# Weight sums of the gate/up turns made by GpSimd additions in place of DVE additions

## The chip, the cores and the metric

The kernel runs on one core of a Trainium2 chip. The metric is the device time of one execution in microseconds (us). TensorE (PE in the profile) multiplies, ScalarE (ACT) and VectorE (DVE) prepare operands, GpSimd (POOL) starts some transfers and does small work, SyncE (SP) starts the loads of the weights.

## The reference, cut to what matters

The model has two layers over 256 tokens of width 2048: a pooling mixer and a SwiGLU FFN, then attention and a SwiGLU FFN. All is float32. The change touches only the two large products of each FFN, gate and up, each 2048 by 5632:

```python
def swiglu(x, wg, wu, wd):
    return (jax.nn.silu(x @ wg) * (x @ wu)) @ wd
...
h = h + swiglu(rmsnorm(h, ffn_norm[layer]), w_gate[layer], w_up[layer], w_down[layer])
```

## The kernel before, in words

**Products in three passes.** Each float32 weight tile is split: ACT rounds it into `w_hi` (L771), DVE subtracts that from the tile and writes the rest into `w_lo` (L1238), and PE makes hi by hi, lo by hi and hi by lo, one matmul of 512 columns each. The tile of one such step is 128 x 1024 and is called a unit. `w_hi` and `w_lo` are rings of `RING` = 4 units: ACT may round unit n when PE has finished unit n - 4 (`unit_used`), DVE follows ACT (`hi_ready`), PE follows DVE (`unit_ready`).

**Turns.** Columns of gate and up are worked off in 11 blocks of 512. Nine of them in each layer (18 in all) are "sum turns". For two sets s = 0 and 1 of the inner dimension a turn uses a seven-product scheme of the Strassen kind: some products take sums of weight halves instead of the halves themselves. A turn has 22 units in the fixed order below, counted from 0. A unit named `gate` or `up` is plain and costs PE 12 matmuls, every other unit costs 6: 180 matmuls in a turn.

```python
SUM_ORDER = [("B11", 0), ("B11", 1), ("B21", 0), ("gate", 4), ("B21", 1), ("gate", 5), ("B22", 1), ("T1", 1),
             ("B22", 0), ("T1", 0), ("gate", 6), ("gate", 7), ("T3", 0), ("T2", 1), ("T4", 0), ("T2", 0), ("T4", 1),
             ("up", 5), ("T3", 1), ("up", 4), ("up", 6), ("up", 7)]
T_SUMS = [("T2", 1), ("T2", 0), ("T4", 0), ("T4", 1)]
```

**The four sums of a set.** The first, T1, and the third, T3, are made by transfers that accumulate, which GpSimd starts (L2084 and L2087). The second is T2 = T1 + B22 and is written over T1; the fourth is T4 = B21 + T2 and is written over B21. Both are DVE additions of 128 x 1024 elements, from `raw` into `raw` (`weight_sum`, L1223 for T2 and L1227 for T4). DVE's own program places them: T2 of set 1 after unit 7, T2 of set 0 after unit 10, T4 of set 0 after unit 11, T4 of set 1 after unit 14. ACT waits on the semaphore `t_sum` before it rounds units 13 (T2, 1), 14 (T4, 0), 15 (T2, 0) and 16 (T4, 1).

**The other work of DVE in a turn.** It transposes the block before (`quad_turn`), combines PSUM banks (L1261 to L1297), and makes the low part of the activations (`act_lo`). GpSimd has no work in a turn but the four starts of transfers. SP's loads wait on `unit_ready` of the last unit that reads a slot of `raw`.

Of the kernel before, what the change touches and what calls it, by code (L numbers as in the profile page):

```python
# [28 lines left out]
ALU = mybir.AluOpType  # L29
# [45 lines left out]
SUM_TURNS = NFB - 2  # L75
# [146 lines left out]
AT = {u: n for n, u in enumerate(SUM_ORDER)}  # L222
# [20 lines left out]
def turn_half(form, n):  # L243

    if form in ("gate", "up"):
        return SLOT[form, n // 2], UNITS_D[n][2]
    slot = (SLOT_U if form in ("T3", "B22") else SLOT_G)[n]
    return slot, 2 * C if form in ("B21", "T4", "B22") else 0
# [33 lines left out]
def trunk(nc, x, pool_w, pool_rows, pool_scale, w_kv, w_q, w_o, w_gate, w_up, w_down, final_norm,  # L282
# [12 lines left out]
    with ExitStack() as ctx:  # L295
# [99 lines left out]
        def sem(name):  # L395
            return ctx.enter_context(nc.semaphore(name))
# [3 lines left out]
        unit_ready = sem("unit_ready")  # L400
# [11 lines left out]
        t_sum = sem("t_sum")  # L412
        t1_in = [sem(f"t1_in{n}") for n in range(SUM_SETS)]
# [65 lines left out]
        def sum_units(l, j):  # L479
            return (LAP_GU[l] + 2).units(SUM_UNITS * (j - 1))  # L480
# [6 lines left out]
        def steps_of(j, n):  # L487
            return 1 if j < SUM_TURNS or n + 1 < SUM_UNITS else 1 + SUM_STEPS - SUM_UNITS * SUM_TURNS
# [3 lines left out]
        def sum_done(l, j, unit):  # L492
            return len(T_SUMS) * (SUM_TURNS * l + j - 1) + T_SUMS.index(unit) + 1
# [519 lines left out]
        def _(ve):  # L1013
# [103 lines left out]
            def up_out(l, j):  # L1117
                job = JOB_GU[l] + 2 * j + 1
                pair = (JOB_GU[l] + 1) % 2
                ve.wait_ge(unit_used, turn_lap(l, j).units(2 * UD))  # L1120
                ve.wait_ge(job_out, job)
                for t in range(T):
                    last = nc.vector.scalar_tensor_tensor(out=act[:, t, :], in0=acc[:, 2 * pair + t, :],
                                                          scalar=r[:, t:t + 1], in1=act[:, t, :],
                                                          op0=ALU.mult, op1=ALU.mult)
                last.then_inc(job_out, 1)
# [87 lines left out]
            def weight_half(unit):  # L1214
                slot, off = turn_half(*unit)
                return raw[:, slot, off:off + 2 * C]

            def weight_sum(l, j, form, s):

                c = SUM_TURNS * l + j - 1  # L1220
                if form == "T2":
                    ve.wait_ge(t1_in[s], 16 * (c + 1))
                    nc.vector.tensor_tensor(weight_half(("T2", s)), weight_half(("T1", s)), weight_half(("B22", s)),  # L1223
                                            ALU.add).then_inc(t_sum, 1)
                else:
                    ve.wait_ge(t_sum, sum_done(l, j, ("T2", s)))
                    nc.vector.tensor_tensor(weight_half(("T4", s)), weight_half(("B21", s)), weight_half(("T2", s)),  # L1227
                                            ALU.add).then_inc(t_sum, 1)

            def sum_turn(l, j):  # L1230

                before = sum_units(l, j)
                c = SUM_TURNS * l + j - 1
                gate = JOB_GU[l] % 2
                for n, unit in enumerate(SUM_ORDER):
                    ve.wait_ge(hi_ready, before + n + 1)
                    w = (before + n) % RING
                    nc.vector.tensor_tensor(w_lo[:, w, :], weight_half(unit), w_hi[:, w, :].bitcast(F32),  # L1238
                                            ALU.subtract).then_inc(unit_ready, steps_of(j, n))
                    if n == 2 and j > 1:  # L1240
                        common_up(l, j - 1)
                    if n == 3:
                        if j > 1:
                            common_out(l, j - 1)
                        else:
                            up_out(l, j - 1)
                        quad_turn(l, j - 1, 0)
                    if n == 5:
                        quad_turn(l, j - 1, 1)
                    if n == 7:  # L1250
                        weight_sum(l, j, "T2", 1)
                    if n == 10:
                        weight_sum(l, j, "T2", 0)
                    if n == 11:
                        weight_sum(l, j, "T4", 0)
                    if n == 14:
                        weight_sum(l, j, "T4", 1)
                    if n == 15:
                        ve.wait_ge(unit_used, before + AT["gate", 7] + 1)
                        ve.wait_ge(p1_copied, c + 1)  # L1260
                        nc.vector.tensor_tensor(act[:, 0, :], pair_bank(gate, 0), common[:, 0, :],  # L1261
                                                ALU.add).then_inc(common_step, 1)
                    if n == 17:
                        ve.wait_ge(unit_used, before + AT["T2", 0] + 1)
                        ve.wait_ge(common_step, 4 * c + 1)
                        nc.vector.tensor_tensor(common[:, 0, :], acc[:, P6, :], common[:, 0, :],
                                                ALU.add).then_inc(common_step, 1)
                    if n == 19:
                        act_lo(l, j - 1)
                    if n == 20:  # L1270
                        ve.wait_ge(unit_used, before + AT["T3", 1] + 1)
                        ve.wait_ge(common_step, 4 * c + 2)
                        nc.vector.tensor_tensor(common[:, 1, :], acc[:, P7, :], common[:, 0, :],
                                                ALU.add).then_inc(common_step, 1)
                    if n == 21:
                        ve.wait_ge(unit_used, before + AT["T4", 1] + 1)
                        ve.wait_ge(common_step, 4 * c + 3)
                        nc.vector.tensor_tensor(act[:, 1, :], pair_bank(gate, 1), common[:, 1, :],
                                                ALU.add).then_inc(gate_sum, 1)
                        ve.wait_ge(gate_sum, c + 1)  # L1280
                        nc.vector.tensor_tensor(common[:, :, :], acc[:, P5:P5 + 1, :].to_broadcast([P, T, C]),
                                                common[:, :, :], ALU.subtract).then_inc(sums_free, 1)

            def common_up(l, j):

                ve.wait_ge(unit_used, sum_units(l, j + 1))
                ve.wait_ge(sums_free, (SUM_TURNS + 1) * l + j + 1)
                up = (JOB_GU[l] + 1) % 2
                nc.vector.tensor_tensor(common[:, :, :], acc[:, 2 * up:2 * up + 2, :], common[:, :, :],
                                        ALU.add).then_inc(common_step, 1)  # L1290

            def common_out(l, j):

                ve.wait_ge(common_step, 4 * (SUM_TURNS * l + j))
                ve.wait_ge(job_out, JOB_GU[l] + 2 * j + 1)
                for t in range(T):
                    last = nc.vector.scalar_tensor_tensor(out=act[:, t, :], in0=common[:, t, :],  # L1297
                                                          scalar=r[:, t:t + 1], in1=act[:, t, :],
                                                          op0=ALU.mult, op1=ALU.mult)
                last.then_inc(job_out, 1)  # L1300
# [163 lines left out]
            for j in range(1, NFB - 1):  # L1464
                sum_turn(0, j)
# [580 lines left out]
        def _(gp):  # L2046
# [26 lines left out]
            def turn_sums(l):  # L2073

                def half(form, s):
                    slot, off = turn_half(form, s)
                    return raw[:, slot, off:off + 2 * C]

                for j in range(1, NFB - 1):
                    before, c = sum_units(l, j), SUM_TURNS * l + j - 1  # L2080
                    for s in (1, 0):
                        gp.wait_ge(unit_ready, before + AT["B11", s] + 1)
                        gp.wait_ge(raw_in[SLOT_U[s]], 16 * sum_loads(l, j, "up", s))
                        gp.dma_start(half("T1", s), half("T3", s), accum_op=ALU.add).then_inc(t1_in[s], 16)  # L2084
                    for s in (0, 1):
                        gp.wait_ge(t1_in[s], 16 * (c + 1))
                        gp.dma_start(half("T3", s), half("B22", s), accum_op=ALU.add).then_inc(t3_in[s], 16)  # L2087

            def rotate(z, heads, n):

# [79 lines left out]
```

## Time and profile before

| what | value |
| --- | --- |
| median of 3 runs | 1667.57 us (1667.55 to 1669.52) |
| the profiled execution, its own time | 1667.48 us |
| its span, first to last instruction | 1665.7 us |
| TensorE busy in the span | 1650.5 us |
| DVE busy | 1414.6 us |
| ACT busy | 1115.3 us |
| GpSimd busy | 96.4 us |
| mean granted TensorE clock | 0.998 |

The 1.8 us between span and time lie around the program. The profiled execution stands 0.09 us under the median. Busy time counts overlapping instructions of an engine once. A timeline row that ends in "x2" is two instructions of one line merged; its duration is the time that the two together cover. Where an engine was idle before a row, the bracket says how long and what ended it.

### The profile page before, as it was taken

To read this page: it belongs to the slowest core of one execution; us is meant where nothing else is said; L and a number is where in the kernel's file an instruction comes from. 1 tells how busy PE (TensorE), PEld (TensorE's weight loads), DVE (VectorE), ACT (ScalarE), POOL (GpSimd) and SP (SyncE) were. 2 spreads that over 40 slices of the span, in tenths; PEclk is the share of its full clock that TensorE was granted. 3 is DMA by queue.
4 is the path that set the end of the run, shared out by engine and by line. 5 is a ranking of instruction groups with operands and counts; after the bars stand their busy time and mean duration, and the time that the engine had idled before them with its cause. 6 is when DMAs were issued, how large, how long until landed. Compare 5 with 4: busy or idle time off the path is not lost.

```text
span 1665.7 us, 19672 instructions
## 1 busy us (share of the span) xinstructions
PE 1650.5 (99%) x7492; PEld 1358.3 (82%) x7492; DVE 1414.6 (85%) x1582; ACT 1115.3 (67%) x1575; POOL 96.4 (6%) x126
## 2 busy tenths in 40 slices
PE   9999999999999999999999999999999999999998
PEld 8878888888888888888777887888888888888887
DVE  7879999999968988867676867999999996889887
ACT  6667777777766555546665565777777776655554
POOL 1100000000000000002011000000000000000000
PEclk9999999999999999999999999999999999999999
DMA  8568888888865565655434556888888887557564
GB/s 294 187 190 258 269 261 261 259 261 260 237 232 172 184 228 190 213 201 179 150 127 152 177 186 193 252 252 253 254 257 259 262 259 249 160 195 236 168 212 167
DMA packets 173590, 364.73 MB, mean 219 GB/s; under 512 B 6708, under 2 KB 6836, under 8 KB 173368
## 3 DMA queue, kind: packets, MB, share of 16 engines
q1 hardware_dynamic: 162832, 324.67, 57.1%
q0 software_dynamic: 10368, 37.75, 12.0%
q8 instruction: 59, 0.97, 0.2%
q10 hardware_dynamic: 296, 1.06, 0.2%
q14 instruction: 35, 0.29, 0.1%
HBM read 323.61 MB, written 2.10 MB: 196 GB/s over the span
## 4 chain that ended last, share of the span: by engine, by line
PE 94%; DMA 2%; DVE 2%; ACT 1%; issue 0%; SPq 0%; ACTq 0%
PE acc L1779 8%; PE acc L1781 8%; PE acc L1780 8%; PE acc L1656 7%; PE acc L1658 7%; PE acc L1657 7%; PE acc L1877 7%; PE acc L1878 7%; PE acc L1879 7%; PE acc L1794 6%; PE acc L1792 6%; PE acc L1793 6%; PE acc L1863 2%; PE acc L1864 2%; PE acc L1862 2%; DMA raw<-w_gate_in 1%
## 5 line engine op out<-in xcount | busy, mean ns | idle before, releaser
L1238 DVE TENSOR_TENSOR w_lo<-raw,w_hi 128x1024 fp32r<-128x1024 f32 x396 | 472.1, 1216 | 41.0 <-ACT w_hi L771 37.1
L771 ACT ACTIVATE w_hi<-raw 128x1024 fp32r<-128x1024 f32 x396 | 412.6, 1058 | 116.4 <-PE acc L1781 59.6
L826 ACT ACTIVATE w_hi<-raw 128x1024 fp32r<-128x1024 f32 x215 | 227.5, 1061 | 190.7 <-PE acc L1879 124.1
L1416 DVE TENSOR_TENSOR w_lo<-raw,w_hi 128x1024 fp32r<-128x1024 f32 x215 | 260.5, 1221 | 60.0 <-ACT w_hi L826 54.8
L1779 PE MATMUL acc<-w_hi,xT_hi 128*128 128x512 f32 x576 | 225.0, 391 | 3.9 <-DVE w_lo L1238 3.9
L1780 PE MATMUL acc<-w_lo,xT_hi 128*128 128x512 f32 x576 | 224.8, 390 | 0.0
L1781 PE MATMUL acc<-w_hi,xT_lo 128*128 128x512 f32 x576 | 224.6, 390 | 0.0
L1877 PE MATMUL acc<-w_hi,hT_hi 128*128 128x512 f32 x488 | 190.1, 390 | 0.3 <-DVE w_lo L1416 0.3
L1879 PE MATMUL acc<-w_hi,hT_lo 128*128 128x512 f32 x488 | 189.8, 389 | 0.0
L1878 PE MATMUL acc<-w_lo,hT_hi 128*128 128x512 f32 x488 | 189.8, 389 | 0.0
L1019 DVE TENSOR_TENSOR w_lo<-raw,w_hi 128x1024 fp32r<-128x1024 f32 x104 | 127.4, 1232 | 66.3 <-ACT w_hi L626 66.1
L1656 PE MATMUL acc<-w_hi,xT_hi 128*128 128x512 f32 x416 | 164.2, 395 | 0.0
L1658 PE MATMUL acc<-w_hi,xT_lo 128*128 128x512 f32 x416 | 162.1, 390 | 0.0
L1657 PE MATMUL acc<-w_lo,xT_hi 128*128 128x512 f32 x416 | 161.9, 389 | 0.0
L626 ACT ACTIVATE w_hi<-raw 128x1024 fp32r<-128x1024 f32 x104 | 108.9, 1062 | 73.2 <-PE acc L1658 56.1
L668 ACT ACTIVATE hT_f<-quad 32x256 f32<-32x256 f32 x320 | 132.8, 415 | 16.0 <-DVE quad L1180 11.2
L1779 PEld LDWEIGHTS acc<-w_hi,xT_hi 128*128 128x128 f32 x576 | 108.5, 188 | 27.4 <-DVE w_lo L1238 4.9
L1780 PEld LDWEIGHTS acc<-w_lo,xT_hi 128*128 128x128 f32 x576 | 108.5, 188 | 22.6
L1781 PEld LDWEIGHTS acc<-w_hi,xT_lo 128*128 128x128 f32 x576 | 108.6, 188 | 22.6
L1792 PE MATMUL acc<-w_hi,s_hi 128*128 128x512 f32 x288 | 112.0, 389 | 0.0
L1793 PE MATMUL acc<-w_lo,s_hi 128*128 128x512 f32 x288 | 112.0, 389 | 0.0
L1794 PE MATMUL acc<-w_hi,s_lo 128*128 128x512 f32 x288 | 112.0, 389 | 0.0
(202 smaller groups left out, 2751.7 us busy)
## 6 DMA issues: line engine op xcount, KB each, us to landing
raw<-w_gate_in SPq DMA_DIRECT2D x88, 1024.0 KB, 7.4
raw<-w_up_in SPq DMA_DIRECT2D x88, 1024.0 KB, 5.3
raw<-w_down_in SPq DMA_DIRECT2D x88, 1024.0 KB, 5.1
raw<-raw POOLq DMA_DIRECT2D x72, 512.0 KB, 5.2
raw<-w_q_in SPq DMA_DIRECT2D x16, 1024.0 KB, 5.1
raw<-w_o_in SPq DMA_DIRECT2D x16, 1024.0 KB, 5.0
raw<-w_kv_in SPq DMA_DIRECT2D x4, 1024.0 KB, 5.3
raw<-pool_w_in SPq DMA_DIRECT2D x3, 1024.0 KB, 13.9
```

Source lines behind the costliest of these rows:

```text
L771: nc.scalar.activation(w_hi[:, (before + n) % RING, :], raw[:, slot, off:off + 2 * C], ACT.Copy).then_inc(hi_ready, steps_of(j, n))
L1238: nc.vector.tensor_tensor(w_lo[:, w, :], weight_half(unit), w_hi[:, w, :].bitcast(F32), ALU.subtract).then_inc(unit_ready, steps_of(j, n))
L1416: nc.vector.tensor_tensor(w_lo[:, n % RING, :], src, w_hi[:, n % RING, :].bitcast(F32), ALU.subtract).then_inc(unit_ready, plan.steps_of(n))
L1656: nc.tensor.matmul(dst, at_hi[:, k, tok], w_hi[:, w, cols], start=first and kk == 0, stop=False)
L1657: nc.tensor.matmul(dst, at_hi[:, k, tok], w_lo[:, w, cols], start=False, stop=False)
L1658: last = nc.tensor.matmul(dst, at_lo[:, k, tok], w_hi[:, w, cols], start=False, stop=end)
L1779: nc.tensor.matmul(dst, xT_hi[:, k, tok], w_hi[:, w, cols], start=start and kk == 0, stop=False)
L1780: nc.tensor.matmul(dst, xT_hi[:, k, tok], w_lo[:, w, cols], start=False, stop=False)
L1781: last = nc.tensor.matmul(dst, xT_lo[:, k, tok], w_hi[:, w, cols], start=False, stop=stop and kk == 1)
L1877: nc.tensor.matmul(dst, hT_hi[:, k, tok], w_hi[:, n % RING, cols], start=start, stop=False)
L1878: nc.tensor.matmul(dst, hT_hi[:, k, tok], w_lo[:, n % RING, cols], start=False, stop=False)
L1879: last = nc.tensor.matmul(dst, hT_lo[:, k, tok], w_hi[:, n % RING, cols], start=False, stop=stop)
```

## The change

`weight_sum` and its four calls leave DVE's program. GpSimd makes the same four additions, in the order of `T_SUMS`, behind the two transfers of T3 that it starts in the same turn. For T2 it waits until DVE has finished `w_lo` of the T1 unit; for T4 it waits for `w_lo` of the B21 unit and for its own T2. Sizes, places and semaphore counts stay.

```diff
@@ -1215,18 +1215,6 @@
-            def weight_sum(l, j, form, s):
-
-                c = SUM_TURNS * l + j - 1
-                if form == "T2":
-                    ve.wait_ge(t1_in[s], 16 * (c + 1))
-                    nc.vector.tensor_tensor(weight_half(("T2", s)), weight_half(("T1", s)), weight_half(("B22", s)),
-                                            ALU.add).then_inc(t_sum, 1)
-                else:
-                    ve.wait_ge(t_sum, sum_done(l, j, ("T2", s)))
-                    nc.vector.tensor_tensor(weight_half(("T4", s)), weight_half(("B21", s)), weight_half(("T2", s)),
-                                            ALU.add).then_inc(t_sum, 1)
@@ -1247,14 +1235,6 @@
-                    if n == 7:
-                        weight_sum(l, j, "T2", 1)
-                    if n == 10:
-                        weight_sum(l, j, "T2", 0)
-                    if n == 11:
-                        weight_sum(l, j, "T4", 0)
-                    if n == 14:
-                        weight_sum(l, j, "T4", 1)
@@ -2085,6 +2065,13 @@
                     for s in (0, 1):
                         gp.wait_ge(t1_in[s], 16 * (c + 1))
                         gp.dma_start(half("T3", s), half("B22", s), accum_op=ALU.add).then_inc(t3_in[s], 16)
+                    for s in (1, 0):
+                        gp.wait_ge(unit_ready, before + AT["T1", s] + 1)
+                        nc.gpsimd.tensor_tensor(half("T2", s), half("T1", s), half("B22", s), ALU.add).then_inc(t_sum, 1)
+                    for s in (0, 1):
+                        gp.wait_ge(unit_ready, before + AT["B21", s] + 1)
+                        gp.wait_ge(t_sum, sum_done(l, j, ("T2", s)))
+                        nc.gpsimd.tensor_tensor(half("T4", s), half("B21", s), half("T2", s), ALU.add).then_inc(t_sum, 1)
```

## Rows read from the trace of the kernel before

**Rows 1.** The page: busy time and instructions of each engine.

```profile
PE 1650.5 (99%) x7492; PEld 1358.3 (82%) x7492; DVE 1414.6 (85%) x1582; ACT 1115.3 (67%) x1575; POOL 96.4 (6%) x126
```

**Rows 2.** Waits of TensorE: us in total, times, longest.

```profile
PE acc L1779 <- DVE w_lo L1238: 3.9, 2, 2.0
```

**Rows 3.** The page's groups by line: busy us, mean ns, idle before.

```profile
L1238 DVE TENSOR_TENSOR w_lo<-raw,w_hi 128x1024 fp32r<-128x1024 f32 x396 | 472.1, 1216 | 41.0 <-ACT w_hi L771 37.1
...
L1227 DVE TENSOR_TENSOR raw<-raw 128x1024 f32<-128x1024 f32 x36 | 43.8, 1218 | 0.0
```

**Rows 4.** Windows: PE, PEld, DVE, ACT, POOL busy; clock, DMA share, GB/s.

```profile
299.00:340.00 41.00, 41.00 (x183) 33.95 (x182) 38.98 (x38) 32.32 (x43) 3.35 (x4) 1.00 0.85 256
```

**Rows 5.** Timelines of one turn, DVE, ACT, POOL, PE: start, us, engine, line.

```profile
306.52 1.22 DVE L1223 TENSOR_TENSOR raw<-raw 128x1024 f32<-128x1024 f32 x1
307.66 1.21 DVE L1238 TENSOR_TENSOR w_lo<-raw,w_hi 128x1024 fp32r<-128x1024 f32 x1
309.05 2.58 DVE L1238 TENSOR_TENSOR w_lo<-raw,w_hi 128x1024 fp32r<-128x1024 f32 x2 [0.17 <-ACT w_hi L771]
...
307.95 1.06 ACT L771 ACTIVATE w_hi<-raw 128x1024 fp32r<-128x1024 f32 x1 [0.34 <-PE acc L1781]
309.31 1.06 ACT L771 ACTIVATE w_hi<-raw 128x1024 fp32r<-128x1024 f32 x1 [0.29 <-PE acc L1794]
...
311.26 1.06 ACT L771 ACTIVATE w_hi<-raw 128x1024 fp32r<-128x1024 f32 x1
...
314.05 3.13 ACT L771 ACTIVATE w_hi<-raw 128x1024 fp32r<-128x1024 f32 x3
...
306.33 1.78 POOL L2087 DMA_DIRECT2D raw<-raw  x2 [5.28 <-DMA raw<-raw]
...
307.75 0.39 PE L1792 MATMUL acc<-w_hi,s_hi 128*128 128x512 f32 x1
...
309.11 0.39 PE L1792 MATMUL acc<-w_hi,s_hi 128*128 128x512 f32 x1
```

**Rows 6.** Timeline of GpSimd: additions of two inputs with VectorE idle or done.

```profile
762.15 0.47 POOL L2097 TENSOR_TENSOR rope_a<-k_dup,ropes 128x128 f32<-128x128 f32 x1 [331.70 <-ACT v_all L897]
762.57 0.32 POOL L2098 TENSOR_TENSOR rope_b<-k_dup,ropes 128x64 f32<-128x64 f32 x1
...
874.13 0.46 POOL L2097 TENSOR_TENSOR rope_a<-q,ropes 128x128 f32<-128x128 f32 x1 [26.18 <-ACT q L886]
```

**Rows 7.** Timelines of VectorE and GpSimd where GpSimd copies beside `w_lo`.

```profile
44.78 3.19 DVE L1019 TENSOR_TENSOR w_lo<-raw,w_hi 128x1024 fp32r<-128x1024 f32 x2
...
44.98 1.91 POOL L2067 COPY h<-hblk 128x1024 f32<-128x1024 f32 x1 [5.17 <-DVE hblk L1067]
...
51.86 2.35 DVE L1019 TENSOR_TENSOR w_lo<-raw,w_hi 128x1024 fp32r<-128x1024 f32 x2
...
52.06 3.04 POOL L2067 COPY h<-hblk 128x1024 f32<-128x1024 f32 x1 [5.17 <-DVE hblk L1067]
```

**Rows 8.** All writers of `w_lo`: duration ns min/median/max, first and last start.

```profile
L1238 DVE TENSOR_TENSOR w_lo<-raw,w_hi x396: 1180/1217/1227, 83.4 to 1378.6; 128x1024 fp32r<-128x1024 f32 x198
...
L1019 DVE TENSOR_TENSOR w_lo<-raw,w_hi x104: 1181/1225/1881, 14.0 to 1419.7; 128x1024 fp32r<-128x1024 f32 x104
```

**Rows 9.** Timeline of a wait of TensorE, and windows around both waits.

```profile
1031.83 1.23 DVE L1238 TENSOR_TENSOR w_lo<-raw,w_hi 128x1024 fp32r<-128x1024 f32 x1 [3.74 <-ACT w_hi L771]
...
1033.11 0.71 PE L1779 MATMUL acc<-w_hi,xT_hi 128*128 128x512 f32 x1 [1.94 <-DVE w_lo L1238]
...
1032.00:1034.00 2.00, 0.90 (x2) 0.74 (x3) 2.00 (x2) 1.95 (x4) 0.00 (x0) 0.81 0.00 0
1034.00:1036.00 2.00, 2.00 (x6) 1.58 (x5) 2.00 (x3) 1.95 (x5) 0.00 (x0) 0.50 0.00 0
1036.00:1038.00 2.00, 2.00 (x9) 1.56 (x8) 1.90 (x3) 1.73 (x3) 0.00 (x0) 0.84 0.63 152
...
108.00:110.00 2.00, 1.24 (x5) 1.05 (x6) 2.00 (x3) 1.95 (x4) 0.00 (x0) 1.00 0.00 0
```

## The prediction

> **What bounds the kernel now.** I read the page first. TensorE is busy 1650.5 of 1665.7 us [rows 1], so the kernel goes as fast as matmuls are fed. The waits of TensorE come next: of all its waits, those in the gate/up turns are two, 3.9 us together [rows 2]. Both are in the first sum turn of a layer, at unit 10, and before the second VectorE itself had been idle for 3.74 us, waiting for ACT [rows 9], so an eased VectorE doesn't shorten them. Then the load of VectorE where the change acts. In a window of 41.0 us, which is one turn, it is busy 38.98 us, ACT 32.32, GpSimd 3.35 [rows 4]. So TensorE sets the pace, and VectorE has 2 us of room in a turn. The reader is to see two things here: nothing is to be won while TensorE never waits, and VectorE is near enough to its limit that a small burden on it shows at once.
>
> The pace of a turn comes from the timelines [rows 5]. Units 6 and 7 start on TensorE at 307.75 and 309.11: 1.36 us for 6 matmuls, so 2.72 for 12 and 40.8 for the 180 of a turn. From 309.11 the other starts follow: unit 8 at 310.47, 9 at 311.83, 10 at 313.19, 11 at 315.91, 12 at 318.63, 13 at 319.99, 14 at 321.35. I call these the due times of `w_lo`. VectorE's pitch for two instructions without a gap is 307.66 - 306.52 = 1.14 us.
>
> **What is removed.** Two additions of T2 and two of T4 in each of 18 turns, 72 in all, at 1.218 us each [rows 3], with the pitch 1.14 us worth 4.6 us in a turn. This is taken from an engine that TensorE waits for only 3.9 us in the whole program, and those two waits aren't of its making. So the removal gains 0.
>
> **What is added.** 72 GpSimd additions of 128 x 1024. No such instruction is in the trace. The nearest are GpSimd multiplications of two inputs with 128 and 64 elements in a row: 0.47 or 0.46 against 0.32 us [rows 6]. The slope is 2.3 or 2.2 ns per element, and 0.32 + 960 x slope gives 2.6 or 2.4 us. I take 2.4. The lower bound is the copy with one input, 128 x 1024: in [rows 7] it ends at 46.89, and the VectorE instruction of 44.78 ends near 46.00, so it needs 0.9 us once it may run. The upper bound is 2.6. The Trainium skill, page "GPSIMD Engine Reference", section on performance versus the Vector engine, gives 4497 ns for 2048 elements, which makes 2.25 us for 1024 an estimate; by that, three additions in the chain below would each be 0.15 us shorter, some 8 us less over 18 turns.
>
> GpSimd has the time: 4 x 2.4 = 9.6 us beside its 3.35 us in 41. The question is what the additions do to VectorE.
>
> **What they do to VectorE.** The copies answer it [rows 7]. The first one starts at 44.98, beside two `w_lo` instructions that cover 3.19 us instead of the 2.35 us that the same pair covers at 51.86. That is 0.84 us more, about the copy's own 0.9. At 52.06 it is the other way round: the VectorE pair runs undisturbed and the copy takes 3.04 us, the rest of the pair and its own 0.9. So a GpSimd instruction that reads SBUF and a VectorE instruction with two SBUF inputs don't run together here; one waits for the whole of the other. The extremes agree: among the 396 `w_lo` of the sum turns, where GpSimd only starts transfers, none is over 1227 ns, but L1019 has one of 1881 [rows 8]. All 22 `w_lo` of a turn have two SBUF inputs; the combinations of PSUM banks and the transposes don't.
>
> The balance of a turn is then 38.98 - 4.6 + 9.6 = 44.0 us of VectorE's time in 40.8 (a little of it hidden where VectorE was idle or reads PSUM). This alone says 3 us longer.
>
> **The walk through the turn of [rows 5].** I let the two take turns where both are waiting, as at 44.98.
> - GpSimd has started both T3 transfers at 306.33 + 1.78 = 308.1. Unit 7 is ready since 306.6, so T2 of set 1 runs 308.1 to 310.5. VectorE did unit 8 before that, as T2 no longer delays it. Unit 9 is rounded at 309.0, is held until 310.5 and done at 311.65; due 311.83. Just in time.
> - T2 of set 0 waits for unit 9. Unit 10, rounded at 310.4, is already running, till 312.8. T2 runs 312.8 to 315.2. Unit 11 (rounded 312.3) is done at 316.4; due 315.9. TensorE waits 0.5.
> - T4 of set 0 comes in behind unit 11, 316.4 to 318.8. Unit 12 (rounded 315.1) is done at 319.95; due 318.63 + 0.5. It waits 0.8 more.
> - T4 of set 1 comes in behind unit 12, 319.9 to 322.3. Unit 13 is done at 323.45; due 321.3 with the delay so far. It waits 2.15 more.
> - Behind it no GpSimd work is left. VectorE's 1.14 us a unit against TensorE's 1.36 keeps up, and the turn ends late by 0.5 + 0.8 + 2.15 = 3.5 us. ACT has T4 of set 0 at 318.8 and of set 1 at 322.3, early enough.
>
> Nothing gives this back: TensorE is busy for the rest of the turn. SP's loads wait on `unit_ready` and move along; the next T1 transfers on GpSimd's queue come some 15 us after the last addition, so what is queued behind the additions isn't late. The waits that ACT had on `t_sum` are covered by its place up to four units ahead of TensorE; if that cover is gone, the stall shows there instead, with the same price.
>
> **The clock.** A wait of 1.94 us at 1033.11 was followed by windows with the granted clock at 0.81, 0.50 and 0.84 [rows 9], that is, down to the 1.2 GHz level for part of 6 us: 2 x (0.19 + 0.50 + 0.16) = 1.7 us lost. The like wait at 108 us left it at 1.00. One of two, for waits of 2 us. The longest piece in the walk is 2.15, so I add half of 1.7, 0.85 us in a turn; the bounds are 0 and 1.7.
>
> **The sum.** 3.5 + 0.85 = 4.35 us in 18 turns is 78 us. In the first turn of each layer two of the additions fall into the wait that is there already, so I take 2 us off for each: 74. To the profiled execution's 1667.48 us, which is within 0.1 of the median, 74 makes 1741; I say 1740.
>
> **The rivals.**
> - Hidden after all, no change: the engines share without harm and TensorE never waits. Then T2 of set 0 ends at 312.8, T4 of set 0 at 315.3 (ACT wants it at 316.1 [rows 5]) and T4 of set 1 at 317.7, before ACT has come two units further. Time 1667.5, and no gain, since TensorE was never held by these additions. For it: GpSimd has the time. Against it: the stretched pair [rows 7]. It decides where two-input additions hold VectorE under some 1 us each. Chance 0.07.
> - Mild: an addition holds VectorE for 1.8 us or less, between the copy's 0.9 and my 2.4. With 1.8 the same walk gives T2 of set 0 312.2 to 314.0, T4 315.15 to 316.95, T4 of set 1 behind unit 12, 318.1 to 319.9, and unit 13 at 321.05, 1.06 late. 18 x 1.06 = 19 us: 1687. The measured slope speaks against it, but those instructions have short runs of 8 and 16 elements, and long ones may go faster. Chance 0.15.
> - VectorE goes first whenever its next unit is rounded, as at 52.06. T2 of set 0 then runs 313.9 to 316.3, T4 of set 0 318.6 to 321.0, T4 of set 1 at once behind it to 323.4, with unit 14, rounded at 322.1, held to 324.65; due 321.35. One wait of 3.3 us, and the clock falls most times: 5.0 x 18 = 90, 1757. This is the same cause in another order, and I count it to the forecast: chance of both together 0.68, range 1715 to 1770.
> - Worse: additions slower than 2.6 us, or a fallen clock and late units meeting in one more wait per turn, over 5.7 us in a turn: over 1770. Chance 0.10.
>
> **How the numbers follow.** The range for 8 in 10 takes the forecast with both orders and the mild case down to a price of 1 us in a turn: 1685 to 1770. Faster by over 0.2% (3.3 us, about what a measurement of this kernel can tell from no change) has nothing to come from: 0.02. Within 0.2%: most of the hidden case, 0.06. Slower: 0.92.
>
> **What would show it.** In the profile after: `w_lo` of L1238 with a maximum near 3.6 us instead of 1.227; GpSimd additions of 2.4 us and, where they wait, up to 3.6; VectorE busy in a turn at 40 us or more, though it has four instructions less; waits of TensorE on `w_lo` of some 3 us in each of 18 turns, at units 11 to 14; windows with a clock under 1.00 in about half of the turns. Wrong it would be if the additions are done within 1.5 us, or if `w_lo` keeps its 1.22 us beside them.

## The result and the profile after

The changed kernel takes 1730.53 us (median of 4 runs, 1728.54 to 1734.45) against 1668.48 us before: a ratio of 1.0378, 95% interval 1.0361 to 1.0394. It is slower by 62 us, where the forecast was 1740 us with a range of 1685 to 1770. The profiled execution took 1730.07 us with a span of 1728.3 us, 62.6 us more than before.

The page after, busy time, chain and groups (L1226 is the `w_lo` line that was L1238; L1759 and L1772 are the gate/up and the sum-form matmuls, L1779 and L1792 before):

```profile
PE 1670.6 (97%) x7492; PEld 1355.9 (78%) x7492; DVE 1481.6 (86%) x1510; ACT 1116.8 (65%) x1575; POOL 313.8 (18%) x198
...
PE 78%; DVE 16%; ACT 3%; DMA 2%; issue 1%; SPq 0%; ACTq 0%
...
L1226 DVE TENSOR_TENSOR w_lo<-raw,w_hi 128x1024 fp32r<-128x1024 f32 x396 | 619.8, 1602 | 40.7 <-ACT w_hi L771 40.7
...
L2070 POOL TENSOR_TENSOR raw<-raw 128x1024 f32<-128x1024 f32 x36 | 110.7, 3075 | 33.9 <-DVE w_lo L1226 33.9
```

VectorE has 72 instructions fewer and is busy 67 us longer than in [rows 1]. All that it gained is in one line: the same 396 `w_lo` cover 619.8 us instead of 472.1 [rows 3], 148 us more, against some 80 us that its own additions had taken. TensorE waits for them, where before it had two waits [rows 2]. Waits of TensorE after: us in total, times, longest.

```profile
PE acc L1772 <- DVE w_lo L1226: 38.3, 43, 1.7
PE acc L1759 <- DVE w_lo L1226: 8.0, 2, 4.0
```

The writers of `w_lo` after (duration min/median/max) show a maximum of 4455 ns where [rows 8] had 1227:

```profile
L1226 DVE TENSOR_TENSOR w_lo<-raw,w_hi x396: 1181/1216/4455, 82.9 to 1441.5; 128x1024 fp32r<-128x1024 f32 x198
```

One turn after, in the timelines of GpSimd, VectorE and TensorE. It answers to [rows 5].

```profile
190.71 1.77 POOL L2067 DMA_DIRECT2D raw<-raw  x2 [4.50 <-DMA raw<-raw]
191.86 3.07 POOL L2070 TENSOR_TENSOR raw<-raw 128x1024 f32<-128x1024 f32 x1
196.09 3.32 POOL L2070 TENSOR_TENSOR raw<-raw 128x1024 f32<-128x1024 f32 x1 [1.17 <-DVE w_lo L1226]
199.56 6.52 POOL L2074 TENSOR_TENSOR raw<-raw 128x1024 f32<-128x1024 f32 x2
...
193.20 16.23 DVE L1226 TENSOR_TENSOR w_lo<-raw,w_hi 128x1024 fp32r<-128x1024 f32 x7 [1.04 <-ACT w_hi L771]
...
200.06 0.39 PE L1761 MATMUL acc<-w_hi,xT_lo 128*128 128x512 f32 x1
200.56 0.50 PE L1759 MATMUL acc<-w_hi,xT_hi 128*128 128x512 f32 x1
...
203.18 0.39 PE L1761 MATMUL acc<-w_hi,xT_lo 128*128 128x512 f32 x1
203.88 0.50 PE L1772 MATMUL acc<-w_hi,s_hi 128*128 128x512 f32 x1 [0.31 <-DVE w_lo L1226]
...
205.15 0.39 PE L1774 MATMUL acc<-w_hi,s_lo 128*128 128x512 f32 x1
207.21 0.50 PE L1772 MATMUL acc<-w_hi,s_hi 128*128 128x512 f32 x1 [1.68 <-DVE w_lo L1226]
```

Seven `w_lo` in a row take 16.23 us; at the undisturbed pitch they would take some 8.1. The matmuls start 0.227 us apart when nothing is missing. What a distance is over that, I call the lateness of a unit: 200.56 - 200.06 - 0.23 = 0.27 at unit 11, 0.47 at unit 12, 1.83 at unit 13, and 0.1 more in each case at the second matmul. The bracket shows less, since it counts only from the end of the matmul before, whose record is 0.39 us long.

### The profile page after: what moved, and what is told of

The parts are those of the page before. It is cut to its first block, busy times and chain, and to the rows that moved or that the text cites. A ratio compares the mean times of both kernels' runs of the same rounds, so it can differ in the third digit from the quotient of the medians.

```text
span 1728.3 us, 19708 instructions
## 1 busy us (share of the span) xinstructions
PE 1670.6 (97%) x7492; PEld 1355.9 (78%) x7492; DVE 1481.6 (86%) x1510; ACT 1116.8 (65%) x1575; POOL 313.8 (18%) x198
## 4 chain that ended last, share of the span: by engine, by line
PE 78%; DVE 16%; ACT 3%; DMA 2%; issue 1%; SPq 0%; ACTq 0%
DVE w_lo L1226 14%; PE acc L1636 7%; PE acc L1638 7%; PE acc L1637 7%; PE acc L1857 6%; PE acc L1858 6%; PE acc L1859 6%; PE acc L1759 6%; PE acc L1761 6%; PE acc L1760 6%; PE acc L1772 4%; PE acc L1773 4%; PE acc L1774 4%; PE acc L1843 2%; PE acc L1842 2%; PE acc L1844 2%
## 5 line engine op out<-in xcount | busy, mean ns | idle before, releaser
L1226 DVE TENSOR_TENSOR w_lo<-raw,w_hi 128x1024 fp32r<-128x1024 f32 x396 | 619.8, 1602 | 40.7 <-ACT w_hi L771 40.7
L1396 DVE TENSOR_TENSOR w_lo<-raw,w_hi 128x1024 fp32r<-128x1024 f32 x215 | 260.5, 1222 | 59.6 <-ACT w_hi L826 54.4
L1759 PE MATMUL acc<-w_hi,xT_hi 128*128 128x512 f32 x576 | 227.9, 396 | 9.0 <-DVE w_lo L1226 8.0
L1019 DVE TENSOR_TENSOR w_lo<-raw,w_hi 128x1024 fp32r<-128x1024 f32 x104 | 127.5, 1233 | 66.4 <-ACT w_hi L626 66.1
L1772 PE MATMUL acc<-w_hi,s_hi 128*128 128x512 f32 x288 | 117.4, 408 | 38.3 <-DVE w_lo L1226 38.3
L1759 PEld LDWEIGHTS acc<-w_hi,xT_hi 128*128 128x128 f32 x576 | 109.1, 189 | 38.3 <-DVE w_lo L1226 15.9
L2064 POOL DMA_DIRECT2D raw<-raw x36 | 31.6, 879 | 536.0 <-DMA raw<-w_up_in 343.0
L2070 POOL TENSOR_TENSOR raw<-raw 128x1024 f32<-128x1024 f32 x36 | 110.7, 3075 | 33.9 <-DVE w_lo L1226 33.9
```

Source lines behind the costliest of these rows:

```text
L1396: nc.vector.tensor_tensor(w_lo[:, n % RING, :], src, w_hi[:, n % RING, :].bitcast(F32), ALU.subtract).then_inc(unit_ready, plan.steps_of(n))
L1759: nc.tensor.matmul(dst, xT_hi[:, k, tok], w_hi[:, w, cols], start=start and kk == 0, stop=False)
```

## The experiments

All times are medians; each ratio is against runs of the kernel before on the same chip.

**1. The additions left out.**

```diff
-                    elif form in ("T2", "T4"):
-                        ac.wait_ge(t_sum, sum_done(l, j, unit))
...
-                    if n == 7:
-                        weight_sum(l, j, "T2", 1)
...
```

> The four additions of a turn are left out and made by nobody (ACT rounds T2 and T4 units from the unsummed halves, so this part of the computation is missing); the rest is the kernel before. Theory, removal gains nothing because TensorE never waited for these additions: 1667.5 us, within 3 us, with VectorE busy some 80 us less. Rival, the relief of VectorE is worth something that the additions then took back: 1655 us or less.

Measured: 1667.22 us, ratio 0.9994 (0.9985 to 1.0003), with VectorE busy 78 us less than before:

```profile
PE 1649.8 (99%) x7492; PEld 1357.6 (82%) x7492; DVE 1336.7 (80%) x1510; ACT 1114.8 (67%) x1575; POOL 96.5 (6%) x126
```

This kernel leaves out the sums T2 and T4. The relief is worth nothing, so the loss of 62 us comes from what was put on GpSimd.

**2 and 3. One kind of addition alone.** Two kernels; in each the sums of one kind are GpSimd's, with a semaphore of their own.

```diff
+                    for s in (1, 0):
+                        gp.wait_ge(unit_ready, before + AT["T1", s] + 1)
+                        nc.gpsimd.tensor_tensor(half("T2", s), half("T1", s), half("B22", s), ALU.add).then_inc(t_sum, 1)
...
+                    for s in (0, 1):
+                        gp.wait_ge(unit_ready, before + AT["B21", s] + 1)
+                        gp.wait_ge(t_sum, sum_done(l, j, ("T2", s)))
+                        nc.gpsimd.tensor_tensor(half("T4", s), half("B21", s), half("T2", s), ALU.add).then_inc(t4_sum, 1)
```

> Only the two T2 additions of a turn are made by GpSimd, the two T4 additions stay on VectorE. Theory, each two-input addition holds w_lo for 2.4 us and TensorE waits once VectorE's lead of 1 to 2 us is used up: unit 9 late by some 0.5 us in the turns where the T3 transfers are started late, unit 11 by 0.4, units 12 to 15 just in time: about 1.0 us in a turn, 18 us, 1686 us (1678 to 1692). Rival, each addition costs a fixed price whatever is beside it: half of the whole loss, 1699 us.

> Only the two T4 additions of a turn are made by GpSimd, the two T2 additions stay on VectorE. Theory: T4 of set 0 runs behind unit 11, unit 12 is just in time, T4 of set 1 comes in behind unit 12 and makes unit 13 late by 0.9 us: 0.9 in a turn, 16 us, 1684 us (1677 to 1692), and no wait at unit 9. Rival with a fixed price per addition: 1699 us.

Measured: T2 alone 1690.26 us, 1.0133 (1.0118 to 1.0149); T4 alone 1688.28 us, 1.0123 (1.0107 to 1.0138). The two add up to 2.6%, the whole change costs 3.8%. Both times lie in their ranges, and the fixed price of 1699 us is out. A part of each addition is absorbed by VectorE's lead, and the second pair finds that lead used up. Unit 9 is late only where T2 of set 1 is on GpSimd, and in the T4 kernel nearly all the lateness is at unit 13, as expected. What I hadn't expected is 0.3 us at unit 16 in the T2 kernel, and that the lateness at unit 13 in the T4 kernel varies, 0.75 to 1.8 us.

**4 to 6. What about an addition holds VectorE.** To the kernel before, with all its sums on VectorE, four GpSimd instructions are added in 16 turns, on constant data; nobody waits for them but GpSimd itself, before its next addition and its next turn. They are additions, copies or memsets.

```diff
+                    for m in range(4 if j < SUM_TURNS else 0):
+                        gp.wait_ge(unit_ready, before + AT["T1", 1 if m == 0 else 0] + 1)
+                        if done + m > 0:
+                            gp.wait_ge(extra, done + m)
+                        nc.gpsimd.tensor_tensor(spare[:, :, :], xT_hi[:, 0:4, :].bitcast(F32), xT_lo[:, 0:4, :].bitcast(F32), ALU.add).then_inc(extra, 1)
```

> The kernel before with all its additions on VectorE, and besides four GpSimd additions of 128 x 1024 in 16 of the 18 turns, at the places of the change, on constant operands, with a result that nobody reads. Theory, the additions cost through what they hold VectorE, not through who waits for their results: VectorE needs 39.0 + 4 x 2.4 = 48.6 us in a turn of 40.8, some of it in its idle time, so about 6 to 7.5 us in a turn: 1765 to 1790 us. Rival, what costs is that ACT waits for slower sums: nobody waits for these, so 1668 us.

> As the run with four extra GpSimd additions in 16 turns on top of the kernel before, but each is a copy of 128 x 1024 with one input. Theory, a GpSimd instruction that reads SBUF holds w_lo for its own length, here 0.9 us: VectorE needs 39.0 + 3.6 = 42.6 us in a turn, less what falls into its idle time: 0.8 to 2 us in a turn, 1681 to 1700 us. Rival, the price is per instruction and not by its length: the same time as with the extra additions.

> As before, but each of the four extra GpSimd instructions is a memset of 128 x 1024, which reads nothing from SBUF. Theory, it is the second input of w_lo that can't be read beside a GpSimd read: 1668 us, within 3 us, and no w_lo over 1.23 us. Rival, any GpSimd instruction on SBUF holds VectorE: longer by its length, 1 us in a turn or more, 1684 us or more.

Measured: additions 1780.67 us, 1.0677 (1.0661 to 1.0693); copies 1696.64 us, 1.0176 (1.0159 to 1.0193); memsets 1668.16 us, 1.0000 (0.9991 to 1.0010). The writers of `w_lo` under additions, copies and memsets, in this order:

```profile
L1240 DVE TENSOR_TENSOR w_lo<-raw,w_hi x396: 1182/1215/4553, 84.6 to 1491.3; 128x1024 fp32r<-128x1024 f32 x198
```

```profile
L1240 DVE TENSOR_TENSOR w_lo<-raw,w_hi x396: 1181/1216/2942, 83.3 to 1407.0; 128x1024 fp32r<-128x1024 f32 x198
```

```profile
L1240 DVE TENSOR_TENSOR w_lo<-raw,w_hi x396: 1180/1218/1228, 85.1 to 1380.9; 128x1024 fp32r<-128x1024 f32 x198
```

All three lie in their ranges. That ACT waits for slower sums isn't needed for the loss: additions that it doesn't wait for cost more than those of the change, since here VectorE still has its own. In the changed kernel too, VectorE's idle time before `w_lo` didn't grow (40.7 us, 41.0 before [rows 3]). The price is that of GpSimd instructions that read: 112 us over 64 additions is 1.8 each (a fallen clock included, 0.984 in the mean), 29 us over 64 copies 0.45, and 64 memsets, each 1.1 us long in the profile, cost nothing. An addition is longer than a copy and reads two inputs instead of one; these runs don't separate the two. By the Trainium skill, page "SBUF — State Buffer", section "Who interferes with whom", a VectorE instruction with two SBUF inputs contends with a GpSimd instruction that reads SBUF and not with one that only writes it; these three runs agree.

**7. Shorter additions.** In the changed kernel each addition is cut into two of 512 columns.

```diff
+                def two_halves(out, a, b, s):
+                    for cols in (slice(0, C), slice(C, 2 * C)):
+                        last = nc.gpsimd.tensor_tensor(half(out, s)[:, cols], half(a, s)[:, cols], half(b, s)[:, cols],
+                                                       ALU.add)
+                    last.then_inc(t_sum, 1)
...
```

> The changed kernel with each of the four GpSimd additions cut into two of 512 columns. Theory, the two engines alternate by instruction, so VectorE gets in after 1.2 us instead of 2.4: w_lo at most some 2.4 us long, units 9, 11, 12 and 13 in time, but the additions end later and units 14 and 15 are 2.0 and 1.0 us late: 3.0 to 3.2 us in a turn, no part at unit 9, about 1720 us (1712 to 1727). Rival, only long single holds hurt: 1690 us or less.

Measured: 1733.26 us, 1.0402 (1.0385 to 1.0419), a miss by 6 us. Units 14 and 15 were late by 1.8 and 0.85 us, with 0.35 more at unit 16, close to the 3.0 expected. But unit 9, which I had at nothing, was late by up to 1.8, and the longest `w_lo` was 4.59 us where I had expected 2.4. The timelines of VectorE and GpSimd in the turn where it was worst:

```profile
235.71 12.24 DVE L1226 TENSOR_TENSOR w_lo<-raw,w_hi 128x1024 fp32r<-128x1024 f32 x5 [0.71 <-ACT w_hi L771]
...
234.71 1.75 POOL L2073 DMA_DIRECT2D raw<-raw  x2 [5.05 <-DMA raw<-raw]
235.86 3.15 POOL L2061 TENSOR_TENSOR raw<-raw 128x512 f32<-128x512 f32 x2
240.19 8.90 POOL L2061 TENSOR_TENSOR raw<-raw 128x512 f32<-128x512 f32 x4 [1.17 <-DVE w_lo L1226]
```

The `w_lo` of unit 9 starts at 235.71, ahead of the additions and 0.75 us before the transfer starts on GpSimd are over (236.46). Yet the next addition, which waits for that `w_lo`, begins only at 240.19. Both halves have run in front of it. So the alternation that my walk assumed doesn't hold at this place.

**8. The first addition ahead of the T3 starts.**

```diff
+                    gp.wait_ge(unit_ready, before + AT["T1", 1] + 1)
+                    nc.gpsimd.tensor_tensor(half("T2", 1), half("T1", 1), half("B22", 1), ALU.add).then_inc(t_sum, 1)
                     for s in (0, 1):
                         gp.wait_ge(t1_in[s], 16 * (c + 1))
                         gp.dma_start(half("T3", s), half("B22", s), accum_op=ALU.add).then_inc(t3_in[s], 16)
...
```

> The changed kernel, but GpSimd makes T2 of set 1 before it starts the two T3 transfers. Theory: unit 9 is late (0.2 to 1.6 us in a turn) because that addition comes behind the T3 starts and meets the w_lo of unit 9. Before them it runs some 1.5 us earlier, between the w_lo of units 7 and 9, so unit 9 loses nothing, or 0.2 at most, and the 0.4, 0.6 and 1.9 us at units 11, 12 and 13 stay: about 0.6 us less in a turn, 1719 us (1714 to 1725). Rival, the late T3 transfers are waited for at unit 12, or the place of the addition doesn't matter: 1730 us or more.

Measured: 1710.70 us, 1.0260 (1.0245 to 1.0276), 3 us better than the range. The lateness at unit 9 is gone, as expected; units 12 and 13 lose 2.5 us as before (in three turns units 10 to 12 lose 3.0 us instead). Two things more came: in most turns unit 11 was no longer late, and the wait at unit 10 of the first turns was gone.

**9. The first addition not queued behind the starts.**

```diff
+                    nc.gpsimd.memset(tick[:, :], 0.0).then_inc(ticked, 1)
+                    gp.wait_ge(ticked, c + 1)
```

> The changed kernel with a memset of 8 columns behind the two T3 starts and a wait on it, so that the first addition reaches the engine only when both starts are done. Theory A, an addition that lies queued behind a start already holds VectorE's second read, so that the w_lo of unit 9, which started before the addition could run, still waits for it: with the addition not queued, unit 9 goes first where it starts first, and the largest lateness of unit 9 (1.6 us) goes away: 1720 to 1727 us, no w_lo over 3.7 us. Theory B, the addition is running in truth when its record begins and the starts are done earlier than recorded: nothing changes but a later first addition: 1730 to 1736 us.

Measured: 1730.37 us, 1.0374 (1.0358 to 1.0390). The time lies in theory B's range and misses theory A's by 3 us. The rows speak the other way. The maximum of `w_lo` fell from 4455 to 3458 ns, and in the turn where unit 9 had been late by 1.6 us its `w_lo` (at 239.52, ahead of the addition) now ran undisturbed:

```profile
239.52 1.23 DVE L1228 TENSOR_TENSOR w_lo<-raw,w_hi 128x1024 fp32r<-128x1024 f32 x1 [0.78 <-ACT w_hi L773]
...
238.36 1.76 POOL L2069 DMA_DIRECT2D raw<-raw  x2 [4.93 <-DMA raw<-raw]
239.48 0.75 POOL L2070 MEMSET tick<- 128x8 f32 x1
240.31 6.04 POOL L2074 TENSOR_TENSOR raw<-raw 128x1024 f32<-128x1024 f32 x2
```

In another turn the `w_lo` of unit 9 began only 0.07 us ahead of the addition, and still it was the addition that waited:

```profile
416.67 1.23 DVE L1228 TENSOR_TENSOR w_lo<-raw,w_hi 128x1024 fp32r<-128x1024 f32 x1 [1.05 <-ACT w_hi L773]
...
416.74 3.42 POOL L2074 TENSOR_TENSOR raw<-raw 128x1024 f32<-128x1024 f32 x1
```

In the changed kernel a `w_lo` that began 0.30 us ahead of the addition's row was held for the whole of it:

```profile
324.79 4.46 DVE L1226 TENSOR_TENSOR w_lo<-raw,w_hi 128x1024 fp32r<-128x1024 f32 x1 [0.17 <-ACT w_hi L771]
...
323.94 1.78 POOL L2067 DMA_DIRECT2D raw<-raw  x2 [4.43 <-DMA raw<-raw]
325.09 3.07 POOL L2070 TENSOR_TENSOR raw<-raw 128x1024 f32<-128x1024 f32 x1
```

This is what theory A says of the mechanism, and its time was wrong for two reasons. The later addition made units 10 and 11 late by 0.6 us each instead, in the turn of 239.52 and five others, and in five more turns unit 9 was still late, by up to 0.8 us. So theory A is likely and not shown; it rests on rows of single turns, here and in run 7, and not on a time.

**10. One addition, early.** The kernel before, and of the four only T4 of set 1 on GpSimd, behind VectorE's T2 of set 1 and ahead of the T3 starts.

```diff
+                    gp.wait_ge(unit_ready, before + AT["B21", 1] + 1)
+                    gp.wait_ge(t_sum, sum_done(l, j, ("T2", 1)))
+                    nc.gpsimd.tensor_tensor(half("T4", 1), half("B21", 1), half("T2", 1), ALU.add).then_inc(t4_sum, 1)
```

> The kernel before with only T4 of set 1 made by GpSimd, at once behind VectorE's T2 of set 1 and ahead of the T3 starts. Theory: it holds VectorE from 307.7 to 310.1 in the turn of the walk, the w_lo of unit 9 is done at 311.3 and due 311.8, the T3 transfers land 2 us later and are still in time: nothing lost, 1668 us (1665 to 1672). Rival, every GpSimd addition costs by its length: a quarter of the loss, 1683 us.

Measured: 1671.59 us, 1.0027 (1.0017 to 1.0036): inside the range, but "nothing lost" was wrong. The timelines of VectorE and GpSimd in one turn:

```profile
225.17 1.22 DVE L1241 TENSOR_TENSOR w_lo<-raw,w_hi 128x1024 fp32r<-128x1024 f32 x1
226.56 4.31 DVE L1241 TENSOR_TENSOR w_lo<-raw,w_hi 128x1024 fp32r<-128x1024 f32 x2 [0.17 <-ACT w_hi L774]
...
225.40 3.25 POOL L2088 TENSOR_TENSOR raw<-raw 128x1024 f32<-128x1024 f32 x1 [5.88 <-DVE raw L1226]
```

I had left out the `w_lo` of unit 8: it goes first, the addition ends at 228.65 instead of some 0.9 us earlier, and unit 9 is 0.55 us late in each of the 18 turns. That alone would be 10 us; the kernel lost 4, because here too the waits at unit 10 of the first turns were gone.

**11 and 12. What this showed of the kernel before.** In runs 8 and 10 GpSimd starts the T3 transfers later. So two kernels with all additions on VectorE and only that changed, once in all turns, once in the first turn of a layer.

```diff
+                    gp.wait_ge(unit_ready, before + AT["B22", 0] + 1)
                     for s in (0, 1):
                         gp.wait_ge(t1_in[s], 16 * (c + 1))
```

> The kernel before, all additions on VectorE, but GpSimd starts the T3 transfers of every turn only when w_lo of unit 8 is done, 2 to 3 us later. Theory, the waits of TensorE at unit 10 in the first turn of a layer (2.4 and 3.8 us there, and smaller ones at times in other turns) come from the T3 transfers sharing the DMA engines with the load of w_gate for units 10 and 11; T3 started behind that load lets it land some 4 us earlier: 1661.5 us (1660 to 1664), no wait at unit 10. Rival, these waits went away in the two runs before because of GpSimd's additions themselves, or T3 now lands too late for unit 12: 1667.5 us or more.

> As the run before, but only in the first turn of each layer, and there the T3 transfers wait for w_lo of unit 9. Theory: the same 1661.5 us (1660 to 1664), since almost all of the waits are in those two turns. If other turns lose by the early T3 too, this one is up to 1 us slower than the run before. Rival: 1667.5 us.

Measured: 1660.94 us, 0.9962 (0.9948 to 0.9976), and 1660.81 us, 0.9960 (0.9946 to 0.9973). Both are 6 us faster than the kernel before and faster than every other version. Timelines of GpSimd, SyncE and ACT in the first turn, before:

```profile
95.44 1.76 POOL L2087 DMA_DIRECT2D raw<-raw  x2 [5.46 <-DMA raw<-raw]
...
97.15 0.37 SPq L560 DMA_DIRECT2D raw<-w_gate_in  x1
...
106.39 1.06 ACT L771 ACTIVATE w_hi<-raw 128x1024 fp32r<-128x1024 f32 x1 [3.94 <-DMA raw<-w_gate_in]
```

and in the first of the two kernels:

```profile
102.31 1.76 POOL L2088 DMA_DIRECT2D raw<-raw  x2 [12.56 <-DVE w_lo L1238]
...
96.90 0.37 SPq L560 DMA_DIRECT2D raw<-w_gate_in  x1
...
102.48 1.06 ACT L771 ACTIVATE w_hi<-raw 128x1024 fp32r<-128x1024 f32 x1 [0.29 <-PE acc L1794]
```

Both times lie in their ranges. The load of `w_gate` is issued at the same place of the turn in both kernels. Issued behind the T3 transfers it lands after 9.2 us, with the T3 transfers started behind it after 5.2, and TensorE has no wait on `w_lo` left. The two runs take the same time, so the T3 starts of the other turns cost nothing.

## Why the prediction was right, step by step

The forecast had its direction and its mechanism right, and its size came out near, 1740 against 1730.5 us. A part of that nearness is luck: two terms were too high and a third was missing. Per step:

- **The removal gains 0.** Shown: leaving the additions out changes nothing (0.9994).
- **An addition takes 2.4 us.** Right: where nothing disturbed it, in the first turn, it took 2.41, 2.39 us:

```profile
99.59 2.41 POOL L2070 TENSOR_TENSOR raw<-raw 128x1024 f32<-128x1024 f32 x1 [2.96 <-DVE w_lo L1226]
104.29 2.39 POOL L2070 TENSOR_TENSOR raw<-raw 128x1024 f32<-128x1024 f32 x1 [2.30 <-DVE w_lo L1226]
```

  The 2.25 us that the prediction estimated from the figure of the Trainium skill (page "GPSIMD Engine Reference", section "Performance versus the Vector engine") are 0.15 too short.
- **It holds `w_lo` for its whole length, and the engines alternate.** Runs 4 to 6 show the hold. Alternation holds from T2 of set 0 on: that addition takes 3.32 us (0.9 of waiting for unit 10) and the two T4 together 6.52 (2 x 2.4 and the rest waiting), as the walk has them. But the hold is 2.2 us and not 2.4. The `w_lo` of units 11, 12 and 13 start 3.36 and 3.32 us apart with an addition between them, where the walk had 1.14 + 2.4 = 3.54:

```profile
197.07 3.43 DVE L1226 TENSOR_TENSOR w_lo<-raw,w_hi 128x1024 fp32r<-128x1024 f32 x1
...
200.43 3.40 DVE L1226 TENSOR_TENSOR w_lo<-raw,w_hi 128x1024 fp32r<-128x1024 f32 x1
...
203.75 3.40 DVE L1226 TENSOR_TENSOR w_lo<-raw,w_hi 128x1024 fp32r<-128x1024 f32 x1
```

- **Late by 0.5, 0.8 and 2.15 us at units 11, 12 and 13.** Right in place, a little too high. Measured in the turn shown, with the tenth at each second matmul: 0.37, 0.58 and 1.94. The walk with a hold of 2.2 us gives 0.25, 0.6 and 2.0. The first varies between 0 and 0.4 from turn to turn, the other two are the same within 0.05 in all 16 turns that aren't a layer's first.
- **Unit 9 just in time.** Wrong in 13 of those 16 turns (at unit 9, or at unit 8 in three of them): up to 1.6 us late, 0.6 in the mean, 10 us in all. In run 8, with the first addition ahead of the T3 starts, the lateness is gone, so that addition's place is the cause. This missing term and the 0.5 us a turn too much at units 11 to 13 nearly cancel: the 3.5 us of the walk stand against 3.59 measured by luck.
- **Half of 1.7 us for the clock.** Mis-sized: it should have been 0 in those 16 turns. A wait with 1.68 us in the bracket leaves the granted clock at 1.00. Windows of the turn's end, and of the first turn of each layer (PE, PEld, DVE, ACT, POOL, clock, DMA share, GB/s):

```profile
206.00:208.00 2.00, 0.79 (x3) 0.67 (x4) 2.00 (x2) 1.06 (x1) 0.07 (x1) 1.00 0.00 0
...
110.00:120.00 10.00, 9.69 (x32) 7.81 (x33) 7.51 (x6) 5.61 (x9) 2.50 (x1) 0.73 0.33 105
1060.00:1070.00 10.00, 6.00 (x23) 4.66 (x22) 7.25 (x4) 6.07 (x10) 7.62 (x3) 0.88 0.29 94
1070.00:1080.00 10.00, 10.00 (x43) 8.18 (x43) 8.51 (x8) 6.45 (x9) 0.44 (x1) 0.94 0.45 127
```

  The clock fell toward its 1.2 GHz level in the first turns alone, behind waits of 4.0 us. One case of two in the trace of before was too thin a base for a price in 18 turns.
- **First turns cheaper by 2 us.** Mis-sized. I took each at 4.35 - 2 = 2.35 us more than before; they were 4.3 and 1.8 us more, 6.1 together against 4.7. Against the 3.59 us of the other turns one was dearer and one cheaper. The `w_lo` of unit 10, already late by its load, was held by a T4 addition on top, and the clock fell.

The sum by what was measured: 16 turns at 3.59 us make 57.5, the two first turns 6.1, together 63.6 us; the spans differ by 62.6. The forecast had 16 x 4.35 + 4.7 = 74. The 10.7 us between are 13.6 too much for the clock and some 9 too much at units 11 to 13, less the 10 that were missing at unit 9 and 1.4 at the first turns.

The rival "hidden after all" falls with runs 4 to 6, "mild" with the 2.2 us of the hold. The order "VectorE goes first" would have shown one wait of 3.3 us at unit 14; the waits are at units 11, 12 and 13. Two of the signs didn't come: the clock stayed at 1.00 in all 16 turns instead of falling in half of them, and the longest `w_lo` was 4.46 us instead of 3.6.

## What to carry to other kernels

Before work is given to an idle GpSimd, look at what it reads and at what VectorE reads meanwhile: in this kernel an addition that costs VectorE 1.14 us held it for 2.2 us on the other engine, and for up to 3.2 us behind transfer starts, so the "relieved" engine ended busier. Count the load of both as one sum (39 - 4.6 + 9.6 us in 40.8) and then walk the units, since only the lead that is really there absorbs a hold. And look at when a queue starts a transfer as well as at what it does: 6 us lay in T3 transfers that were started earlier than anybody needed them, in front of a load that TensorE was waiting for.

## What was not expected of the hardware

- A GpSimd addition that is next in line behind two transfer starts seems to hold VectorE already while the starts run. In 15 of the 16 turns the row of the first addition ends 2.4 us after the starts end, which is its own length, so it works only from there. Yet the `w_lo` at 324.79 (shown under run 9), which began 0.9 us before the starts ended at 325.72, was kept until the addition was over, 4.46 us long. With the addition kept out of the queue the longest was 3.46. What holds VectorE in that time was not measured in itself.
- GpSimd memsets of 128 x 1024, 64 of them, left VectorE's two-input instructions untouched (maximum 1228 ns).
- The clock didn't follow the length of a wait alone. Waits of TensorE of 1.7 us in the bracket, one in each of 16 turns, never lowered it. In the trace of before a wait of 1.94 us did and one of 1.98 us didn't [rows 9]. In run 4 the wait at unit 11, of over 3 us, lowered it in 15 of 16 turns, but not in the first of them, where it was 3.60 us:

```profile
108.76 0.50 PE L1779 MATMUL acc<-w_hi,xT_hi 128*128 128x512 f32 x1 [1.98 <-DVE w_lo L1238]
...
116.95 0.50 PE L1781 MATMUL acc<-w_hi,xT_hi 128*128 128x512 f32 x1 [3.60 <-DVE w_lo L1240]
114.00:126.00 12.00, 9.01 (x38) 7.11 (x39) 12.00 (x10) 6.51 (x11) 1.81 (x1) 1.00 0.37 105
...
211.65 0.80 PE L1781 MATMUL acc<-w_hi,xT_hi 128*128 128x512 f32 x1 [3.13 <-DVE w_lo L1240]
208.00:220.00 12.00, 8.87 (x28) 6.74 (x27) 12.00 (x8) 3.41 (x5) 5.68 (x2) 0.72 0.27 88
```

  The first line is of before, the other four of run 4.
